# Plain fp32 products in place of three fp32r passes, and ten loading slots without splits

## The reference, cut to what matters

```python
# network 1: block 0, then block 1
mix0 = rglru_block(h)   # in 1024->2x1344, conv of 4 taps, block-diagonal gates, scan, out 1344->1024
h = layer_norm(ALPHA * h + mix0)
ff = (silu(h @ Wg) * (h @ Wu)) @ Wd                 # D_FF = 3584
h = layer_norm(ALPHA * h + ff)
mix1 = gla_block(h)     # gated linear attention, in 1024->3088, out 1024->1024, chunks of 64
h = layer_norm(ALPHA * h + mix1)
for e in range(8):      # top 2 of 8 experts, each a SwiGLU with D_FF = 3584
    y = y + gates[:, e:e + 1] * swiglu(h, w_in[e], w_out[e])
h = layer_norm(ALPHA * h + y)[16:]                  # 256 tokens go on
# network 2, modulated by six vectors of c @ w_ada (1024 -> 6144)
h = h + g1 * (attention(norm(h)) @ w_o)             # 8 latent heads, 4 differential heads
h = h + g2 * hmoe(norm(h))                          # top 2 of 4 in one of 4 groups, 16 experts of 512
```

## Time and profile before

| | |
|---|---|
| three runs | 1939.75, 1934.21, 1938.63 us; median 1938.63 |
| the profiled execution | 1938.98 us, of which the span is 1936.9 us |
| busy, of the span | PE 1812.8 us (94%), PE weight loads 1033.9, DVE 607.6, ACT 476.9, POOL 351.6 |
| mean granted PE clock | 0.964 of 2.4 GHz |
| moved by DMA | 582.87 MB, mean 301 GB/s |
| chain that ended last, by engine | PE 73%, DMA 14%, DVE 8%, ACT 3%, issue 1% |

### The profile page before, as it was taken

The page is one execution under the profiler, slowest core; times in us unless marked ns, Lnnn a source line. Parts: engine busy times, 40 slices in busy tenths (PEclk is TensorE's granted clock), DMA queues, the critical chain, the costliest instruction groups (busy, mean ns, idle before and its releaser), DMA issues.

```text
span 1936.9 us, 26926 instructions
## 1 busy us (share of the span) xinstructions
PE 1812.8 (94%) x11141; PEld 1033.9 (53%) x11141; DVE 607.6 (31%) x1227; ACT 476.9 (25%) x799; POOL 351.6 (18%) x306
## 2 busy tenths in 40 slices
PE   7999999999998999999999999999997887699998
PEld 7987999777975333323332333222322886544443
DVE  6777554338466200100010000000001685501112
ACT  5854444325332110000100000000001564321121
POOL 3000000000000699999930000000000000000000
PEclk9998999998998899999999999999999897889999
DMA  6555667446724999999999999999998440569997
GB/s 192 150 146 187 202 199 241 142 141 220 249 89 155 402 418 413 420 419 420 413 419 420 419 412 416 420 419 419 415 420 297 137 158 9 217 275 417 420 420 291
DMA packets 152739, 582.87 MB, mean 301 GB/s; under 512 B 11673, under 2 KB 77866, under 8 KB 109600
## 3 DMA queue, kind: packets, MB, share of 16 engines
q1 hardware_dynamic: 150000, 575.09, 76.4%
q0 software_dynamic: 2608, 5.97, 1.2%
HBM read 579.96 MB, written 1.05 MB: 300 GB/s over the span
## 4 chain that ended last, share of the span: by engine, by line
PE 73%; DMA 14%; DVE 8%; ACT 3%; issue 1%; SPq 0%; ACTq 0%; DVEq 0%
PE ps L1789 17%; DMA ring<-in_moe_w_out 9%; PE ps L437 9%; PE ps L438 8%; PE ps L439 8%; PE ps L2294 6%; PE ps L1782 5%; PE ps L1821 4%; PE ps L2318 3%; DMA ring<-in_moe_w_in 3%; DVE wlo L480 2%; DMA more<-in_moe_w_out 1%; PE ps L1825 1%; DMA more<-in_moe_w_in 1%; PE ps L637 1%
## 5 line engine op out<-in xcount | busy, mean ns | idle before, releaser
L1789 PE MATMUL ps<-ring,xg 128*64 128x512 f32 x1638 | 406.3, 599 | 4.5 <-DMA ring<-in_moe_w_in 2.4
L480 DVE TENSOR_TENSOR wlo<-raw,whi 128x2048 fp32r<-128x2048 f32 (+5 forms) x96 | 211.5, 2207 | 190.0 <-ACT whi L462 189.7
L1789 PEld LDWEIGHTS ps<-ring,xg 128*64 128x64 f32 x1638 | 120.9, 137 | 247.5 <-issue 239.6
L462 ACT ACTIVATE whi<-raw 128x2048 fp32r<-128x2048 f32 (+6 forms) x97 | 178.7, 1846 | 184.7 <-PE ps L439 77.5
L1821 PE MATMUL ps<-ring,ahm 128*64 128x512 f32 x808 | 203.4, 597 | 8.4 <-DMA ring<-in_moe_w_out 8.4
L437 PE MATMUL ps<-xh,whi 128*128 128x272 f32 (+1 forms) x712 | 210.6, 296 | 0.6 <-DVE xl L529 0.6
L439 PE MATMUL ps<-xh,wlo 128*128 128x272 f32 (+1 forms) x712 | 208.8, 293 | 0.0
L438 PE MATMUL ps<-xl,whi 128*128 128x272 f32 (+1 forms) x712 | 208.6, 293 | 0.0
L2219 POOL TENSOR_SCALAR lnt<-lnt,h 128x384 f32<-128x384 f32 x120 | 188.6, 1572 | 12.2
L1962 DVE TENSOR_TENSOR sgm<-sgm,ps 128x512 f32<-128x512 f32 x28 | 17.5, 683 | 495.7 <-PE ps L1789 495.7
L437 PEld LDWEIGHTS ps<-xh,whi 128*128 128x128 f32 (+1 forms) x712 | 133.7, 188 | 4.0 <-issue 2.4
(11 more groups left out here) (586 smaller groups left out, 2439.8 us busy)
## 6 DMA issues: line engine op xcount, KB each, us to landing
ring<-in_moe_w_in SPq DMA_DIRECT2D x117, 1024.0 KB, 19.6
ring<-in_moe_w_out SPq DMA_DIRECT2D x101, 1024.0 KB, 20.1
ring<-in_moe_w_in SPq DMA_DIRECT2D x117, 768.0 KB, 11.9
ring<-in_w_gate SPq DMA_DIRECT2D x29, 1024.0 KB, 14.2
raw<-in_ffn_w_in SPq DMA_DIRECT2D x28, 1024.0 KB
ring<-in_w_down SPq DMA_DIRECT2D x26, 1024.0 KB, 12.9
raw<-in_w_ada SPq DMA_DIRECT2D x24, 1024.0 KB
ring<-in_w_up SPq DMA_DIRECT2D x20, 1024.0 KB, 9.9
```

The lines of the kernel that those rows point to most:

```text
L462: e.activation(whi[0:rows, s % NSPL, 0:n], raw[0:rows, i % NRAW, 0:n], ACT.Copy).then_inc(S.hi.s, S.hi.up((s,)))
L480: e.tensor_tensor(wlo[0:rows, s % NSPL, 0:n], raw[0:rows, i % NRAW, 0:n], whi[0:rows, s % NSPL, 0:n].bitcast(F32), ALU.subtract).then_inc( ...
L1789: ins = e.matmul(ps_[b][64 * v:64 * v + 64, :], a[:, j, 64 * v:64 * v + 64], both[v][:, 0, 512 * b:512 * b + 512], start=j == 0, stop=j == 7)
```

## The change

Every `mm3` becomes one plain fp32 `matmul` of the unsplit operands. `split_hi`, `split_half`, `split_lo`, `xl`, `xch`, `xcl`, `fal`, `fam` and the parts' slots go; `M` loads straight into ten slots, the whole former area. Each turn's drains are dealt by turns, even `k` to DVE, odd `k` to ACT. In both expert layers one plain product of `hh` with `sel` (read as fp32) stands for the two fp32r ones; `hh` stays ACT's copy, `hl` goes, and PE waits for ACT's second copy in its place. The slots are handed to the rings in a new order. The expert products themselves, the modulation products and the attention stay.

```diff
-NRAW, NSPL = 4, 3
+NRAW = 10
-    ring = right("ring", [128, NRAW + 2 * NSPL, CW])
+    ring = right("ring", [128, NRAW, CW])
+    xh = xg
-    def mm3(e, o, lh, ll, rh, rl, start, stop):
-        e.matmul(o, lh, rh, start=start, stop=False)
-        e.matmul(o, lh, rl, start=False, stop=False)
-        return e.matmul(o, ll, rh, start=False, stop=stop)
     def weights(e, S, key):
-        e.wait_ge(S.lo.s, S.lo.at(s))
-        return whi[0:rows, s % NSPL, 0:n], wlo[0:rows, s % NSPL, 0:n]
+        e.wait_ge(S.raw[i % NRAW].s, S.raw[i % NRAW].at(i))
+        return ring[0:rows, i % NRAW, 0:n]
     def load_chunks(e, S, begin, end):
             if first <= i < first + NRAW:
-                e.wait_ge(pe.s, pe.at("ring", R1.name, last_in(ring[:, 2 * NSPL + k, :])))
+                e.wait_ge(pe.s, pe.at("ring", R1.name, last_in(ring[:, k, :])))
             if i >= NRAW:
-                p = S.chunks[i - NRAW][4]
-                if p is None or i - NRAW in S.kept:
-                    e.wait_ge(S.pe.s, S.pe.at("used", i - NRAW))
-                else:
-                    e.wait_ge(S.lo.s, S.lo.at(p))
+                e.wait_ge(S.pe.s, S.pe.at("used", i - NRAW))
     def act_turn(e, key, tiles, nk, to, gain=None, shift=None):
+        for k in range(1, nk, 2):
+            p, o = bank(key, k)[:, c0:c1], to[:, k, c0:c1]
             e.wait_ge(pe.s, pe.at(key, "T", k))
+            if shift is not None:
+                e.activation(o, p, ACT.Identity, bias=shift(k), scale=gain(k)).then_inc(act.s, act.up((key, "x", k)))
     def dve_turn(e, key, tiles, nk, to, gain=None, shift=None):
+        for k in range(0, nk, 2):
+            if shift is not None:
+                e.tensor_scalar(o, p, gain(k), shift(k), ALU.mult, ALU.add).then_inc(dve.s, dve.up((key, "x", k)))
     def pe_rg_in(e, key, back):
-                    ins = mm3(e, p, wh[:, k, 112 * i:112 * i + 112], wl[:, k, 112 * i:112 * i + 112], xh[:, k, :], xl[:, k, :],
-                              k == 0, k == 7)
+                    ins = e.matmul(p, w[:, k, 112 * i:112 * i + 112], xh[:, k, :], start=k == 0, stop=k == 7)
     def pe_ffn(e):
-                            e.wait_ge(dve.s, dve.at("x1", "lo", k))
+                            wait_x(e, "x1", k)
-                        ins = mm3(e, p, wh[:, k, 128 * i:128 * i + 128], wl[:, k, 128 * i:128 * i + 128], xh[:, k, :], xl[:, k, :],
+                        ins = e.matmul(p, w[:, k, 128 * i:128 * i + 128], xh[:, k, :], start=k == 0, stop=k == 7)
     def dve_ffn(e):
-                e.tensor_tensor(g, g, bank("fu", f)[:, 0:T], ALU.mult).then_inc(dve.s, dve.up(("fu", f)))
-                e.wait_ge(act.s, act.at("fa", f))
-                e.tensor_tensor(fal[:, f, :], g, fah[:, f, :].bitcast(F32), ALU.subtract).then_inc(dve.s, dve.up())
-                e.tensor_copy(fam[:, f, :], g[:, 0:32]).then_inc(dve.s, dve.up(("fa", f)))
+                e.tensor_tensor(fa[:, f, :], g, bank("fu", f)[:, 0:T], ALU.mult).then_inc(dve.s, dve.up(("fu", f), ("fa", f)))
+    def ring_slots(order, more, end):
+        out = [(ring[:, i % NRAW, :], ((pe, "used", i),)) for i in order]
+    LAST1 = chunk_at(*(("ada", j) for j in (16, 17, 18)), ("go", 2), ("go", 3), *(("ada", j) for j in range(19, 24)))
+    LAST2 = list(range(len(M.chunks) - NRAW, len(M.chunks)))
         def part(x, i):                                   # pe_first, and alike in pe_pairs
-                    e.matmul(o, w["hh"][:, t, a:a + 128], sel[:, t, 0:160], start=t == 0, stop=False)
-                    ins = e.matmul(o, w["hl"][:, t, a:a + 128], sel[:, t, 0:160], start=False, stop=t == 1)
+                    ins = e.matmul(o, w["hh"][:, t, a:a + 128], sel[:, t, 0:160].bitcast(F32), start=t == 0, stop=t == 1)
-        e.wait_ge(dve.s, dve.at("m1", "hl"))
+        e.wait_ge(act.s, act.at("m1", "hh", 1))
-        dve_moe_parts(e, "m1", lambda t: w1["hh"][:, t, :], lambda t: w1["hl"][:, t, :], lambda t: h[:, t, :], (0,))
         dve_order(e)
```

More of the change, by code:

```diff
@@ L120, with __init__, add @@
 class Stream:
[L123 to L134, removed]
+    def __init__(self, raw, pe, name=""):
+        self.raw, self.pe, self.name = raw, pe, name
+        self.chunks, self.index = [], {}
+    def add(self, key, rows, n, pieces, zero=False):
+        self.index[key] = len(self.chunks)
+        self.chunks.append((key, rows, n, pieces, zero))
     def again(self):
-        for sig in (*self.raw, *((self.hi, self.lo) if self.hi is not None else ())):
+        for sig in self.raw:
             sig.n = 0
@@ L150, in build @@
         "posr", "relb", "small", "br", "out")}
-    M = Stream([Sig(sem(f"s_raw{i}_in")) for i in range(NRAW)], Sig(sem("s_hi")), Sig(sem("s_lo")), pe)
+    M = Stream([Sig(sem(f"s_raw{i}_in")) for i in range(NRAW)], pe)
     cst = sb("cst", [128, C_END])
[L156 to L162, removed]
     with ExitStack() as own:
@@ L204, in plan_ada @@
             part = w_ada[256 * (j % 4):256 * (j % 4) + 256, 1024 * (j // 4):1024 * (j // 4) + 1024]
-            M.add(("ada", j), 128, CW, by_rows(part, 0, 2, 1024), split=False)
+            M.add(("ada", j), 128, CW, by_rows(part, 0, 2, 1024))
     def gate_pieces(j):
@@ L292, in plan_pairs @@
                     for u in range(2):
-                        S.add((key, x, nm, j, u), 128, CW, rows_of(d[n][0, 2 * x + u], j, 2 if nm == "d" else 4), split=False)
-    R1 = Stream([Sig(sem(f"s_first{i}_in")) for i in range(NRING1)], None, None, pe, "first")
+                        S.add((key, x, nm, j, u), 128, CW, rows_of(d[n][0, 2 * x + u], j, 2 if nm == "d" else 4))
+    R1 = Stream([Sig(sem(f"s_first{i}_in")) for i in range(NRING1)], pe, "first")
     plan_first(R1, "m1")
-    R2 = Stream([Sig(sem(f"s_ring{i}_in")) for i in range(NRING)], None, None, pe, "second")
+    R2 = Stream([Sig(sem(f"s_ring{i}_in")) for i in range(NRING)], pe, "second")
     plan_pairs(R2, "m2")
@@ L496, in load_chunks @@
             if zero:
                 e.wait_ge(pool.s, pool.at("zero", i))
-            slot = raw[0:rows, k, 0:n]
+            slot = ring[0:rows, k, 0:n]
             for dst, src in pieces(slot):
@@ L709, in by_turns, with wait_x, pe_turn_tiles @@
         return (act if k % 2 else dve, key, "x", k)
[L711 to L723 removed]
+    def wait_x(e, key, k):
+        sig, *mark = by_turns(key, k)
+        e.wait_ge(sig.s, sig.at(*mark))
+    def pe_turn_tiles(e, key, norm, tiles, nk, ahead):
         p = {}
@@ L1470, in dve_gla @@
         dve_ada(e, 3)
-        for j in range(6):
-            split_lo(e, M, s)
-            s += 1
         for ch in range(4):
@@ L2223, in pool_rel @@
         pool.label(("round_m1",))
-    SLOTS = ring_slots("wo", len(M.chunks), [more[:, i, :] for i in range(2)], "end_mid") + [(xslot[:, 0:CW], ((pe, "m2", "logits"),))]
+    SLOTS = ring_slots(LAST2, [more[:, i, :] for i in range(2)], "end_mid") + [(xslot[:, 0:CW], ((pe, "m2", "logits"),))]
     NP = 8
@@ L3039, in dve_mid @@
         dve_angles(e)
-        for j in range(3):
-            split_lo(e, M, s)
-            s += 1
         for t in range(2):
```

512 lines of the change are left out of this document (117 added, 395 removed).

## The result

Four runs of the changed kernel took 2025.8 to 2030.2 us, median 2028.36; the kernel before took 1937.86 in its four runs there. The ratio is 1.047, 95% interval 1.0447 to 1.049. Forecast were 2044 us and a range of 2016 to 2064: the direction and the range held, the loss was 90 us where 105 were forecast. A second set of runs of the changed kernel gave 2027.52 and 1.049 (1.0461 to 1.0521).

A forecast was written before the change was run, and what follows sets the result against it. PE was taken to bound everything up to the routing, weight loads the first expert layer. Terms 107 - 8 + 0 + 0 + 5.4 + 0.5 = +105 us on 1936.9, plus 2.1, gave 2044 us; range 2016 to 2064.

The forecast's parts named there:

- The price of a product: TensorE's plain product: two records, 0.229 us each at 272 columns, 0.433 at 512; +107 us up to the routing.
- Step 2: Up to the routing: waits for splits, drains and low parts come back, -8 us, between -3 and -20.
- Step 3: First expert layer: fixed by its weights at 418 GB/s, cost 0; 4 us if the cover were gone.
- Step 4: Attention chunk loads after the first expert layer start 19 us later; cost 0, at most 10 us.
- Step 5: Attention stage: dearer products less waits for splits and turns, +5.4 us, between -8 and +17.
- Step 6: Second expert layer: 32 records of 0.112 us in place of 32 passes of 0.111, +0.5 us over eight pairs.
- Rival (b): Splits brake every stage more than PE's waits show: 20 us back before routing, 12 more in attention; 2020 us; 14%.

The follow-up runs named there:

- the first experiment: Kernel before with every three-pass product made one plain fp32 product, all splits and both gathers kept: 2045.93 us, ratio 1.0569.
- six slots ahead: Changed kernel with SyncE waiting for the use of the chunk six before, not ten, in all but the expert stream: 2041.95 us, ratio 1.0548.
- the one with the plain output product: Kernel before with both gathers plain and `wo` plain, its four chunks and two turns unsplit: 1926.09 us (0.9953), again 1927.96 us (0.996).

## Why the forecast was right, and where it was off

- **The price of a product** was right to a percent: 0.229 and 0.436 us a record against 0.229 and 0.433, +104.7 us up to the routing with the splits kept against 107. This is the mechanism that decides the case, and the first experiment shows it stage by stage.
- **Step 2** gave back 8.2 us up to the router (718.55 to 710.32) and 0.8 to the expert load where I had 8 in all, but in another coin: from the kernel with splits kept to the changed one, the clock lost in the four stages fell from 17.0 to 11.9 us (windows of 2 us summed; from 14.1 to 10.7 if only PE's busy time counts). So 3 to 5 us were clock, for which I had booked about 1. That the sum came out is partly luck.
- **Step 3** was right: from the first expert load to the last down product 860.1 us, in place of 860.8.
- **Step 4** was right, cost 0: late loads, no wait.
- **Step 5** is the mis-sized term. Inputs and scores: +6.3 and then -2.4 were forecast; the inputs stage is +3.9, and from first scores to first output product it is -9.1. DVE does read the scores early now, as forecast. The pauses of 1.8 and 2.5 us are gone, and most of the lower clock with them: that stretch lost 11.5 us to the clock before, 1.7 after (windows of 4 us summed); less that, its length is 38.6 and 39.3 us. I had booked time at the lower clock as a part of 5.7 us in the inputs and none in the scores. But the splits explain little of it. With all of them kept and only the products plain the stretch is already down to 46.8 us and 6.8 lost: the slower products leave DVE time to be done, and the pause of 2.5 is 0.45. And with the changed kernel's pauses of 0.3 and 2.2 us the stretch took anything from 41.0 to 46.3 us and lost 1.7 to 8.5 in seven profiles, 45.9 and 6.8 with six slots ahead. So of the 9.1 us some 4 went with the pauses, and as much as 5 can be the pattern that this program happened to meet. The output's stage was +1.2 for +1.5 forecast.
- **Step 6**: +0.5 forecast, -3.2 measured from second gather to the end, nearly all of it clock (0.50 in the gather before, 0.77 after).
- Sum: in the profiled executions the forecast missed 17.2 us (+87.8 for +105). Of these 3.3 lie ahead of the first expert load (99 forecast, 95.7 measured), 3.1 between it and the first scores (+6.3, +3.2), 10.7 behind them (-0.4, -11.1). Rival (b), more stalls in each stage, had the right sign. Its 12 us up to the routing came to 3.3, its 12 in the attention stage to 9.4 (-4.0 for +5.4), and the time of 2028 lies between its 2020 and the forecast's 2044. Its reason, splits as the brake, is not what the runs show for the scores: the pause went with the splits kept, and the rest of the gain there can be the clock's pattern. Shifted by some 7 us the same program takes 3.3 more there. The price is no luck; how far the sum missed behind the scores is, in part.

## What to carry to other kernels

Where PE sets the pace, count its passes: four plain ones lose to three of split operands by the columns streamed, whatever DVE and ACT save. Plain is the better form where a product is at the floor of 0.11 us a pass anyway (the gathers) or, as the pause at the scores suggests, where a split stands right ahead of something PE waits for (`wo`). Before trusting a difference of a few us in a stretch where PE sets the pace, take length times (1 - granted clock) off both sides; where it doesn't, the clock costs less than that, or nothing.

## What the runs showed that I had not expected

- Length times (1 - granted clock) was 70 us before and 40 after. Of the 23 us that the kernel with plain products won outside the first expert layer by losing its splits and low copies, 14 to 19 were clock.
- The clock falls or not behind equal pauses (0.3 to 2.2 us) and equal busy shares: 1.00, 0.58 and 0.51 in three kernels; a stretch of 41 us differs by 5 for that alone. What decides it beyond position in time stays open: the changed kernel repeated its 41.0 us, the one with the plain output product took 44.2 and 45.9.
- The same code up to the first expert product took 625.9 to 631.9 us in the five profiles with three passes there and the plain gather; in them the recurrent block took 158.2 to 161.3 us and lost 3.5 to 6.6 of it to the clock.
